# Loading x turned, and applying the first norm's factors to the products of a two-block transformer kernel

## What is computed

```python
def rmsnorm(x, g):
    y = x * rsqrt(mean(x * x, axis=-1) + 1e-6)      # one factor for each token
    return y * g                                    # g: one gain for each feature

hn = rmsnorm(x, norm_g)
z = hn @ w_in                                       # 1024 x 4252, split into:
(aq, ak, av, ag, mq, mk, mv, mo, mi, mf, mg, gq, gk, gv, ga, gg) = split(z)
# aq, ak, av: attention, width 384; its output is multiplied by silu(ag)
# mq, mk: silu of a causal convolution of 4 taps over the tokens; mv, mo, mi, mf, mg: mLSTM
# gq, gk, gv, ga, gg: gated linear attention
```

## Time and profile before

| | |
|---|---|
| median of 3 runs | 1566.72 us |
| lowest to highest | 1566.24 to 1569.39 us |
| the profiled execution | 1568.99 us, span of its instructions 1567.3 us |
| TensorE matmul busy | 1531.5 us, 98% of the span |
| VectorE, ScalarE, GpSimd busy | 826.5, 721.6, 318.6 us |
| DMA | 127.99 MB, mean 82 GB/s |

### The profile page before, as it was taken

One profiled execution on the slowest core, in us unless ns is written; L12 is line 12 of the kernel. 1 busy time (PEld: TensorE's weight loads), 2 busy tenths in 40 slices (PEclk: granted clock), 3 DMA queues, 4 the chain that ended last, 5 costly groups with the idle time before them and its releaser, 6 DMA issues. The chain is left out here.

```text
span 1567.3 us, 22091 instructions
## 1 busy us (share of the span) xinstructions
PE 1531.5 (98%) x8990; PEld 1294.3 (83%) x8990; DVE 826.5 (53%) x1412; ACT 721.6 (46%) x1404; POOL 318.6 (20%) x273
## 2 busy tenths in 40 slices
PE   7999999999999999999999999999999999999998
PEld 6888788998898887888888888678887888888887
DVE  5336656556445755845234443668956544244442
ACT  4335645465654644534124443567844443134431
POOL 1000142001430001344014431032001433024420
PEclk9999999999999999999999999989999999999999
DMA  7211112323220003333223332110012333223331
GB/s 245 68 58 64 55 54 89 129 68 108 83 93 28 28 1 108 92 97 121 93 81 95 99 111 86 37 45 15 15 67 81 102 100 120 82 81 98 114 101 51
DMA packets 37518, 127.99 MB, mean 82 GB/s; under 512 B 4248, under 2 KB 8872, under 8 KB 37416
## 3 DMA queue, kind: packets, MB, share of 16 engines
q1 hardware_dynamic: 37416, 126.57, 25.2%
HBM read 124.46 MB, written 2.10 MB: 81 GB/s over the span
## 5 line engine op out<-in xcount | busy, mean ns | idle before, releaser
L321 PE MATMUL bank<-hhi,whi 128*128 128x512 f32 x1056 | 415.8, 394 | 4.5 <-ACT hhi L1973 1.8
L323 PE MATMUL bank<-hhi,wlo 128*128 128x512 f32 x1056 | 411.8, 390 | 0.0
L322 PE MATMUL bank<-hlo,whi 128*128 128x512 f32 x1056 | 411.8, 390 | 0.0
L312 DVE TENSOR_TENSOR wlo<-wstage,whi 128x1024 fp32r<-128x1024 f32 (+10 forms) x250 | 278.4, 1116 | 110.2 <-ACT whi L302 109.9
L302 ACT CAST whi<-wstage 128x1024 fp32r<-128x1024 f32 (+10 forms) x250 | 236.0, 948 | 136.9 <-PE bank L323 131.9
L2458 DVE SCALAR_TENSOR_TENSOR cr<-bank,vc,cr 128x511 f32<-128x511 f32 (+1 forms) x168 | 125.8, 749 | 217.1 <-ACT cr L2397 214.1
L321 PEld LDWEIGHTS bank<-hhi,whi 128*128 128x128 f32 x1056 | 198.0, 188 | 50.6 <-ACT hhi L1973 4.2
L323 PEld LDWEIGHTS bank<-hhi,wlo 128*128 128x128 f32 x1056 | 198.0, 187 | 42.7
L322 PEld LDWEIGHTS bank<-hlo,whi 128*128 128x128 f32 x1056 | 198.1, 188 | 41.3 <-issue 0.5
L2397 ACT ACTIVATE cr<-bank,vc 128x512 f32<-128x512 f32 x84 | 65.5, 780 | 248.5 <-PE bank L323 248.5
L2503 POOL TENSOR_TENSOR cr<-cr,cr 128x512 f32<-128x512 f32 x44 | 94.2, 2140 | 315.6 <-DVE cr L2458 280.9
(11 more groups left out here) (418 smaller groups left out, 2308.9 us busy)
## 6 DMA issues: line engine op xcount, KB each, us to landing
wstage<-in_wts SPq DMA_DIRECT2D x147, 512.0 KB, 3.5
wstage<-in_wts SPq DMA_DIRECT2D x32, 704.0 KB, 4.1
wstage<-in_wts SPq DMA_DIRECT2D x12, 768.0 KB, 4.4
xT<-in_x SPq DMA_DIRECT2D x4, 512.0 KB, 4.9
xt<-in_x SPq DMA_DIRECT2D x4, 512.0 KB, 6.1
out<-ob SPq DMA_DIRECT2D x8, 256.0 KB, 2.3
U<-in_rel_ext SPq DMA_DIRECT2D x6, 256.0 KB, 9.1
wstage<-in_wts SPq DMA_DIRECT2D x2, 618.0 KB, 3.8
```

Of the source, the lines that this page charges most:

```text
L312: e.tensor_tensor(K.wlo[i % 3][:, p], K.stage[i % 3][:, p], K.whi[i % 3][:, p].bitcast(F32), SUB).then_inc(*K.dve.up(("wlo", i) if last el ...
L321: e.matmul(o, lh, rh, start=start, stop=False)
L322: e.matmul(o, lh, rl, start=False, stop=False)
L323: return e.matmul(o, ll, rh, start=False, stop=stop)
```

## The change

The host adds a turned copy of x to the inputs, `x_turned`, in four pieces of 128 x 2 x 512. SP loads them into `xin`; `hhi` and `hlo` are made from it, without the norm's factors. x itself is loaded behind the first three weight chunks, for the squares and their sums only, which move from the "x" steps into the second "den" step (`act_factors`, `dve_factors`). The turns on TensorE go. TensorE spreads the 512 factors over all partitions by four products with the identity (`pe_factors`), and ScalarE copies them to `rb`. Products that have tokens on the partitions get their factor as a column in the operation that takes them from the bank; those with tokens along the free dimension (aq, ak, mqk, gq, gk) are multiplied by `rb` on VectorE, aq, ak and mqk into one buffer `nt`, from which the halves and the taps are then made. gq moves from ScalarE to VectorE. The steps of aq 0, ak 0 and aq 1 on ScalarE and VectorE shift: the factors take the second "den" step, aq 0 the third, ak 0 and aq 1 share the fourth. Not shown: the silus and exponentials of mo, mg, ag and gg with a column factor, and the products that follow them.

```diff
@@ -512,13 +511,17 @@
 
 def sp_init(e, q, K):
     x = K.d["x"].rearrange("a (c p) n -> p (a c) n", p=P)
+    sp_load(e, q, K)
+    for j in range(4):
+        e.dma_start(K.xin[:, 2 * j:2 * j + 2, :], K.d["x_turned"][j]).then_inc(*K.turned_in[j].up(("xin", j), by=16))
+        if j == 0:
+            e.dma_start(K.vc[:], K.d["vecs"]).then_inc(*K.consts_in.up(by=16))
+            e.dma_start(K.fb[:], K.d["fox_b_f_2"].rearrange("a n -> n a")).then_inc(*K.consts_in.up("consts", by=16))
+        if j == 1:
+            sp_load(e, q, K)
+    sp_load(e, q, K)
     for c in range(4):
         e.dma_start(K.yt[:, c, :], x[:, c, :]).then_inc(*K.x_in[c].up(("x_in", c), by=16))
-        if c == 1:
-            e.dma_start(K.vc[:], K.d["vecs"]).then_inc(*K.consts_in.up(by=16))
-            e.dma_start(K.fb[:], K.d["fox_b_f_2"].rearrange("a n -> n a")).then_inc(*K.consts_in.up("consts", by=16))
-    for _ in range(3):
-        sp_load(e, q, K)
     for hh in range(6):
         src = K.d["rel_ext"][hh:hh + 1, 1:513]
         skew = bass.AP(tensor=src.tensor, offset=src.offset, ap=[[1, P], [1, 512]])
@@ -534,23 +537,38 @@
 
 
 def act_x(e, q, K):
+    yield
+    q.wait_ge(*K.at("consts"))
+    for kt in range(8):
+        q.wait_ge(*K.at(("xin", kt // 2)))
+        e.activation(K.hhi[:, kt, :], K.xin[:, kt, :], ACT.Identity, scale=K.col("norm_g", kt)).then_inc(
+            *K.act.up(("h1", "hi", kt)))
+    yield
+
+
+def dve_x(e, q, K):
+    yield
+    for kt in range(8):
+        q.wait_ge(*K.at(("h1", "hi", kt)))
+        e.scalar_tensor_tensor(out=K.hlo[:, kt, :], in0=K.xin[:, kt, :], scalar=K.col("norm_g", kt), in1=K.hhi[:, kt, :].bitcast(F32),
+                               op0=MUL, op1=SUB).then_inc(*K.dve.up(("h1", "lo", kt)))
+    yield
+
+
+def act_factors(e, q, K):
+
     q.wait_ge(*K.at("epsc"))
     for c in range(4):
         t = K.tmp.take(q, ("x", "junk", c))
         q.wait_ge(*K.at(("x_in", c)))
         e.activation(t[:], K.yt[:, c, 0:512], ACT.Square, accum_out=K.small[:, 2 * c:2 * c + 1]).then_inc(
             *K.act.up(("x", "sq", c), frees=[("x", "junk", c)]))
-        r = K.small[:, 16 + c:17 + c]
-        q.wait_ge(*K.at(("x", "sum", c)))
-        act_rstd(e, q, K, ("x_r", c), r, r, D)
-    yield
-    q.wait_ge(*K.at("consts"))
-    for kt in range(8):
-        act_hi(e, q, K, ("h1", "hi", kt), ("xT", kt), K.hhi[:, kt, :], K.col("norm_g", kt))
-    yield
-
-
-def dve_x(e, q, K):
+    q.wait_ge(*K.at(("x", "sums")))
+    act_rstd(e, q, K, "x_r", K.small[:, 16:20], K.small[:, 16:20], D)
+
+
+def dve_factors(e, q, K):
+
     s = K.small
     for c in range(4):
         xc = K.yt[:, c, 512:1024]
@@ -559,30 +577,38 @@
             q.wait_ge(*K.at(("x", "sq2", c - 1)))
         e.tensor_tensor_reduce(K.hold.buffers[0].t[:], xc, xc, 1.0, 0.0, MUL, ADD, s[:, 2 * c + 1:2 * c + 2]).then_inc(
             *K.dve.up(("x", "sq2", c)))
-        q.wait_ge(*K.at(("x", "sq2", c)))
-        q.wait_ge(*K.at(("x", "sq", c)))
-        e.tensor_tensor(s[:, 16 + c:17 + c], s[:, 2 * c:2 * c + 1], s[:, 2 * c + 1:2 * c + 2], ADD).then_inc(
-            *K.dve.up(("x", "sum", c)))
-        q.wait_ge(*K.at(("x_r", c)))
-        e.tensor_scalar(K.yt[:, c, :], K.yt[:, c, :], s[:, 16 + c:17 + c], None, MUL).then_inc(*K.dve.up(("yt", c)))
-    yield
-    for kt in range(8):
-        dve_lo(e, q, K, ("h1", "lo", kt), ("xT", kt), ("h1", "hi", kt), K.hlo[:, kt, :], K.hhi[:, kt, :],
-               K.col("norm_g", kt))
-    yield
-
-
-def pe_x(e, q, K):
+    q.wait_ge(*K.at(("x", "sq2", 3)))
+    q.wait_ge(*K.at(("x", "sq", 3)))
+    e.tensor_tensor(s[:, 16:20], s[:, 0:8:2], s[:, 1:8:2], ADD).then_inc(*K.dve.up(("x", "sums")))
+    q.wait_ge(*K.at("x_r"))
+    e.tensor_scalar(s[:, 20:24], s[:, 16:20], -1.0, None, MUL).then_inc(*K.dve.up("x_nr"))
+
+
+def pe_factors(e, q, K):
+
+    b = K.RG.take(q, "rb")
     q.wait_ge(*K.at("ident"))
-    yield
-    banks = [(K.RA if kt < 7 else K.STAT).take(q, ("xT", kt)) for kt in range(8)]
+    q.wait_ge(*K.at("x_r"))
     for c in range(4):
-        q.wait_ge(*K.at(("yt", c)))
-        for kt in range(8):
-            z = e.transpose(banks[kt][:, c * P:(c + 1) * P], K.yt[:, c, kt * P:(kt + 1) * P], K.ident[:])
-            if c == 3:
-                z.then_inc(*K.pe.up(("xT", kt)))
-    yield
+        z = e.matmul(b[:, c * P:(c + 1) * P], factor(K, c).to_broadcast([P, P]), K.ident[:], start=True, stop=True)
+    z.then_inc(*K.pe.up("rb"))
+
+
+def factor(K, c, sign=1):
+
+    return K.small[:, 16 + c:17 + c] if sign > 0 else K.small[:, 20 + c:21 + c]
+
+
+def act_factor_evac(e, q, K, name, bank, o, i, c):
+    q.wait_ge(*K.at("x_nr"))
+    q.wait_ge(*K.at(bank))
+    e.activation(o, i, ACT.Identity, scale=factor(K, c)).then_inc(*K.act.up(name, frees=[bank]))
+
+
+def dve_factor_evac(e, q, K, name, bank, o, i, c):
+    q.wait_ge(*K.at("x_nr"))
+    q.wait_ge(*K.at(bank))
+    e.tensor_scalar(o, i, factor(K, c), None, MUL).then_inc(*K.dve.up(name, frees=[bank]))
 
 
 
@@ -599,6 +625,8 @@
 
     for key in (("aq", 0), ("ak", 0)):
         pe_fm(e, q, K, key, x, 8, T, K.RG)
+        if key[0] == "ak":
+            pe_factors(e, q, K)
         yield
     fm(("aq", 1))
     yield
...
@@ act_den @@
 def act_den(e, q, K):
     def aqk(i):
-        act_hi(e, q, K, ("aqh", i), ("aq", i), K.aqh[:, i, :], 0.125)
+        q.wait_ge(*K.at(("n", "aq", i)))
+        e.copy(K.aqh[:, i, :], K.nt["n", "aq", i][:]).then_inc(*K.act.up(("aqh", i)))
 
     def akk(i):
-        act_hi(e, q, K, ("akh", i), ("ak", i), K.akh[:, i, :])
+        q.wait_ge(*K.at(("n", "ak", i)))
+        e.copy(K.akh[:, i, :], K.nt["n", "ak", i][:]).then_inc(*K.act.up(("akh", i)))
 
     def conv(m):
         t = K.tmp.take(q, ("cv", m))
-        q.wait_ge(*K.at(("mqk", m)))
-        e.activation(t[:], K.bank(("mqk", m))[:], ACT.Identity, scale=K.col("conv_w", 4 * m + 3)).then_inc(
+        q.wait_ge(*K.at(("n", "mqk", m)))
+        e.activation(t[:], K.nt["n", "mqk", m][:], ACT.Identity, scale=K.col("conv_w", 4 * m + 3)).then_inc(
             *K.act.up(("cv", m, 0)))
 
     def conv_silu(m):
@@ -704,15 +734,17 @@
         act_sigmoid(e, q, K, ("ce", m), t[:], K.tmp["cv", m][:], ("cv", m, 3))
 
...
     yield
+    act_factors(e, q, K)
+    yield
+    act_evac(e, q, K, "rfac", "rb", K.rb, K.bank("rb")[:])
     aqk(0)
     yield
     akk(0)
-    yield
     aqk(1)
     yield
     for c in range(4):
...
-                e.copy(o, i).then_inc(*K.act.up(("gtok", c) if n else ("gtok", c, 0)))
-            act_evac(e, q, K, ("mva", c), b, K.mva[:, c, :, 0:64],
-                     K.bank(b)[:, 0:384].rearrange("p (h n) -> p h n", h=6))
+                e.activation(o, i, ACT.Identity, scale=factor(K, c)).then_inc(*K.act.up(("gtok", c) if n else ("gtok", c, 0)))
+            act_factor_evac(e, q, K, ("mva", c), b, K.mva[:, c, :, 0:64],
+                            K.bank(b)[:, 0:384].rearrange("p (h n) -> p h n", h=6), c)
...
-    q.wait_ge(*K.at(("att", "fin", 2)))
-    q.wait_ge(*K.at(("gqk", 0)))
-    e.activation(K.gq[:], K.bank(("gqk", 0))[:], ACT.Identity, scale=32 ** -0.5).then_inc(*K.act.up("gq", frees=[("gqk", 0)]))
...
 def dve_den(e, q, K):
+    def normed(key, i, scale):
+        t = K.nt.take(q, ("n", key, i))
+        q.wait_ge(*K.at("rfac"))
+        q.wait_ge(*K.at((key, i)))
+        e.scalar_tensor_tensor(out=t[:], in0=K.bank((key, i))[:], scalar=scale, in1=K.rb, op0=MUL, op1=MUL).then_inc(
+            *K.dve.up(("n", key, i), frees=[(key, i)]))
+        return t
+
     def aqk(i):
-        dve_lo(e, q, K, ("aql", i), ("aq", i), ("aqh", i), K.aql[:, i, :], K.aqh[:, i, :], 0.125)
+        t = normed("aq", i, 0.125)
+        q.wait_ge(*K.at(("aqh", i)))
+        e.tensor_tensor(K.aql[:, i, :], t[:], K.aqh[:, i, :].bitcast(F32), SUB).then_inc(
+            *K.dve.up(("aql", i), frees=[("n", "aq", i)]))
 
     def akk(i):
-        dve_lo(e, q, K, ("akl", i), ("ak", i), ("akh", i), K.akl[:, i, :], K.akh[:, i, :])
+        t = normed("ak", i, 1.0)
+        q.wait_ge(*K.at(("akh", i)))
+        e.tensor_tensor(K.akl[:, i, :], t[:], K.akh[:, i, :].bitcast(F32), SUB).then_inc(
+            *K.dve.up(("akl", i), frees=[("n", "ak", i)]))
 
     def conv(m):
-        b = K.bank(("mqk", m))
+        b = normed("mqk", m, 1.0)
         t = K.tmp["cv", m]
         for s in range(1, 4):
             q.wait_ge(*K.at(("cv", m, s - 1)))
             e.scalar_tensor_tensor(out=t[:, s:T], in0=b[:, 0:T - s], scalar=K.col("conv_w", 4 * m + 3 - s), in1=t[:, s:T],
-                                   op0=MUL, op1=ADD).then_inc(*K.dve.up(("cv", m, s), frees=[("mqk", m)] * (s == 3)))
+                                   op0=MUL, op1=ADD).then_inc(*K.dve.up(("cv", m, s), frees=[("n", "mqk", m)] * (s == 3)))
 
     def conv_silu(m):
         q.wait_ge(*K.at((("ce", m), "sig")))
@@ -819,15 +866,16 @@
             *K.dve.up(("cqk", m), frees=[("cv", m), ("ce", m)]))
 
     yield
+    dve_factors(e, q, K)
+    yield
     aqk(0)
     yield
     akk(0)
-    yield
...
```

(17 more changed lines are left out.)

55 lines of the change are left out of this document (31 added, 24 removed).

## The result

| | before | changed |
|---|---|---|
| median, same chip, 4 runs each | 1568.06 us | 1582.29 us |
| lowest to highest | 1566.24 to 1570.44 us | 1581.62 to 1585.59 us |
| the profiled execution (its span) | 1568.99 us (1567.3) | 1582.61 us (1580.8) |

The ratio is 1.0094, with an interval of 1.0073 to 1.0115: the changed kernel is slower by 14 us, and the time lies inside the range that was given. By the spans of the two profiled executions it is 13.5 us.

A forecast was written before the change was run, and what follows sets the result against it. TensorE, busy 1531.5 of 1567.3 us, was taken to bound the kernel. Terms 8.2 + 1.7 + 1.0 + 0.4 + 1.6 = +12.9 us gave a forecast of 1579.6 us (chance 0.62), range 1573 to 1586.

The forecast's parts named there:

- (a): Opening without turns: first product at about 8.2, ak 0 finished 5.8 us earlier, at about 20.9; nothing reaches the end by itself.
- (b): Start: factors stand behind chunk 3's split, landing at 27.2; TensorE waits some 13 us, aq 1 starts 8.2 us later.
- the sum's reading: Opening transfer queue: chunk 3 lands behind the bytes queued ahead of it, at 27.2, as the forecast total assumes.
- rival C: Opening: chunk 3, issued at about 12.3, does not queue behind other transfers and lands before 19.0; 1563.8 us, chance 0.04.
- (g): Extra scalings, fused factors, gq's move and SP's four more issues: no cost; up to +2 us if ml-stage cover is thin.
- (c): Clock after TensorE's wait for the factors: falls to half rate, +1.7 us, bounds 0 and 3.4.
- (d): Second av tile: aq 1's bank is freed later because VectorE handles ak 0 first, +1.0 us (0.5 to 1.3).
- (e): Evacuations of mv on ScalarE: a column factor lengthens each by 0.1 us, delaying two bank releases, +0.4 us.
- (f): mqk banks: ScalarE's conv waits for VectorE, the gates run late, mqk 4's bank is freed later, +1.6 us (-3.3 to +3).
- rival A: mqk banks: start waits as forecast, but their earlier release wins, -3.3 us there; 1574.7 us, chance 0.16.

The follow-up runs named there:

- busy_wait: Changed kernel with 56 useless products on TensorE where it otherwise waits for the factors; 1583.09 us, ratio 1.0109 to the kernel before.
- loads_only: Changed kernel with weight chunk 3 loaded ahead of the six transfers into U and chunk 4 behind them; 1576.65 us, ratio 1.007 to the kernel before.
- aq1_first: Changed kernel with aq 1 scaled and split ahead of ak 0 on VectorE and ScalarE; 1581.59 us, ratio 1.0089 to the kernel before.
- mqk4_first: Changed kernel with VectorE's scaling of mqk 4 put ahead of the gates' log-sigmoid and scans; 1579.74 us, ratio 1.0088 to the kernel before.
- after_shift24: Changed kernel with twelve small float32 products (24 records), result unused, put first in TensorE's stream; 1584.97 us, ratio 1.011 to the kernel before.

## Why the prediction was right, and where it was not

(a) Right. The early start gives nothing by itself: the first product is at 7.84 (8.2 was put), and the wait before the factors takes it all. The gaps that I expected while the later pieces land did not occur; instead the products ran at half clock up to 14 us, and ak 0 was finished at 21.8, not 20.9. The wait hides this.

(b) Right in mechanism and nearly in size. Chunk 3 was cast at 27.58 (27.2 was put for the landing), TensorE had the factor at 34.9 (34.1), the wait was 13.06 (some 13). The step that was mis-sized most is the last one, four products in 0.8 us; they took 1.70. Nearly all of the difference is the clock, as busy_wait shows with 0.92. Ahead of it 0.8 us were missing: 0.4 in the landing and 0.4 in VectorE's four squares. I took 0.69 each, but each waits for the one before it, and they follow each other every 0.84 us (30.76, 31.60 above). With both, aq 1 shifted by 9.9 instead of 8.2.

Chunk 3's landing of about 27.5 fits the sum's reading that the transfers ahead of it set it; loads_only, with the transfers into U behind it, has it 7.0 us earlier. The earlier issue that rival C counted on did not even occur: SP needed 5.04 us for six transfers into U instead of some 3 before, and issued chunk 3 at 15.56, not 12.3. The four more issues of (g), which were to end before 13 us at no cost, thus came with slower issues behind them; what that cost no run separates.

(c) Right that it falls, 1.4 us in place of 1.7, split between the factor products (0.78) and aq 1 (0.60). (b) and (c) together were put at 9.9 and measured 10.57 at av. The Trainium skill's rule on an idle array ("TensorE: Matmul & The Clock Gate", Part 1) agrees with this wait of 13 us, and with the opening of the changed kernel too, where after 7.8 us of idleness the products start 0.43 us apart, as at half clock. The row with 1.00 that I had set against the rule, as speaking for a term of 0, has no record of the clock behind it: I misread it. The term stood on the gap at 103.57 alone, and that was the right one of the two.

(d) Right: 1.0 was put, the second av tile shifted by 1.15 more than the first, with a wait of 0.97 us. aq1_first shows its cause.

(e) Right: 0.4 was put, the shift grows by 0.55 over the two waits for mv (which are 1.27 and 1.96 us in the changed kernel, in place of 0.98 and 1.68).

(f) The wait was right to a tenth: VectorE begins to scale mqk 4 at 158.26, which less the shift of 12.38 is 145.88, and 145.9 was put. TensorE is late by 1.69 there (1.6 was put; the two times in the prediction, 146.6 and 144.87, give 1.7). The gain of an earlier release (rival A) is refuted, as the bank is released too late by the order on VectorE. What was wrong is that the term ended there. The wait of 3.27 us, 1.37 longer than before, brought a longer stretch at half clock behind it, and by hm the shift had grown by another 1.15; mqk4_first removes wait and stretch together and gets 6.0 us back at hm.

(g) Wrong as "no cost": from hm to yh it takes 1.04 us more. The cover I named was for the extra work of VectorE and ScalarE, and I found no wait on these; what changed in this stretch are the places of the instruction blocks. after_shift24 put them back and won only 0.24 of the 1.04. The 0.80 left is what its gaps marked issue are longer than before's: 1.41, 1.32 and 0.42 us against 1.06, 1.28 and none. Why they are longer at the same places stays open.

Not in the sum: -2.8 us at 1040 to 1060 us. The prediction added to the span of one execution of before in which this stretch was at half clock, and the changed kernel's was not. No run shows that this belongs to the kernels and not to the two executions. 9.88 + 0.69 + 1.15 + 0.11 + 0.55 + 1.69 + 1.15 + 1.04 - 2.8 gives the 13.5 by which the spans differ (12.9 was put). The errors, +3.4 and -2.8, nearly cancel. The median came out 2.7 us above the forecast, of which 1.3 is that before had a higher median beside this kernel (1568.06, not 1566.72). That the total was met so closely is partly luck; that it is slower, and mostly by (b), is not. Rival C was not near: chunk 3 would have had to land before 19.0.

## What to carry to other kernels

When a small computation is moved next to a prefetch on an in-order engine, it inherits the landing of that prefetch; put what the bottleneck engine waits for ahead of the splitting or copying of later weights. A saving is only had if the next thing in the chain is also early: here removing the first wait gave 7 to 9 us, but to be level with the old kernel, or a hair below it, it took three more edits, and part of each gain was lost again to half clock or a gap elsewhere. Follow the shift of the same instructions through both traces; it tells in which stretch a time arises, where totals mix gains and losses of several places. A single trace per kernel does not tell a difference of 3 us in its half-clock stretches from chance. And where a view says full clock, hold the distance of two like products against it.

## What the runs showed of the hardware that I had not expected

- SP's issue of a transfer became slower for a while in the changed kernel: of the six transfers into U the first three took 0.44 to 0.45 us, as most before, the last three 0.89, 1.05 and 1.55, with eleven earlier transfers still under way (5.04 us in all). The number under way is not the cause by itself: from 15.5 to 17 us, with thirteen and fourteen, an issue took 0.43 to 0.53. The cause stays open.
- TensorE stood still for up to 2.95 us at places fixed by the number of its instructions, multiples of 127 products with their loads apart, and only where these had run fast. It went on 1.2 to 1.6 us after a packet of the instruction queue had ended. Adding or removing instructions anywhere ahead moves the products that are hit.
- TensorE ran at half clock at the opening of every kernel here, by the distance of its products (0.43 us for 512 columns), until the trace's first record of the clock (11.5 to 18.0 us), while the view of the clock prints 1.00.
- The clock fell behind some waits of 2 us and not behind others. The wait of 1.97 us for y by the small attention products was followed by 0.50 from 1050 to 1060 us in before; the same wait, 1.97 us, in the changed kernel at 1066 us left the clock at 1.00. What decides between the two, these runs don't tell. It made 2.8 us between these two traces, with no edit in that part; and before, unchanged, differs by 10 us between executions.
- A float32 product of 128 columns takes two records, 0.42 us at half clock and 0.23 at full. Those of 16 columns were no faster: 0.43 each in the first 7 us of after_shift24, at the half clock of the opening (no run has them at full clock).
